# Second attention of a two-block kernel: forget decays as row products of running sums instead of masked decay matrices

## What is computed

```python
qh = rms_norm(heads(q), q_gain); kh = rms_norm(heads(k), k_gain)
logf = jax.nn.log_sigmoid(f_logit + f_bias)          # (B, S, 8)
c = jnp.cumsum(logf, axis=1).transpose(0, 2, 1)      # running sum over tokens
s = einsum('bhtd,bhsd->bhts', qh, kh) * scale
s = s + c[:, :, t, None] - c[:, :, None, s]          # decay between key s and query t
s = where(t >= s, s, -inf); pr = softmax(s); o = pr @ v
```

## Time and profile before

| what | value |
|---|---|
| median of 3 runs | 912.39 us (912.27 to 912.58) |
| the profiled execution's own time | 910.87 us |
| its span in the profile | 909.2 us |
| mean granted clock of TensorE | 0.994 of full speed |
| the stretch of this change in the profile | about 564 to 633 us |

### The profile page before, as it was taken

One profiled execution on the slowest core, in us unless ns is written; L12 is line 12 of the kernel. 1 busy time (PEld: TensorE's weight loads), 2 busy tenths in 40 slices (PEclk: granted clock), 3 DMA queues, 4 the chain that ended last, 5 costly groups with the idle time before them and its releaser, 6 DMA issues.

```text
span 909.2 us, 16558 instructions
## 1 busy us (share of the span) xinstructions
PE 879.7 (97%) x7228; PEld 816.3 (90%) x7228; DVE 626.8 (69%) x758; ACT 482.7 (53%) x578; POOL 43.9 (5%) x66
## 2 busy tenths in 40 slices
PE   8999899998988999999999999989999999999997
PEld 8988899998878999999979888989989999999986
DVE  6879477697938855478887886985466555555564
ACT  5657723647426744367776454565545443443463
POOL 5000150000000000000000000131000000000000
PEclk9999999999988999999999999999999999999999
DMA  9846210324108974579965443351454655555521
GB/s 256 278 167 205 79 50 3 140 94 139 47 1 297 388 270 164 186 271 368 351 207 186 144 161 112 126 195 50 142 185 152 228 188 188 183 185 190 181 93 47
DMA packets 88905, 156.75 MB, mean 172 GB/s; under 512 B 7432, under 2 KB 61184, under 8 KB 84864
## 3 DMA queue, kind: packets, MB, share of 16 engines
q1 hardware_dynamic: 88144, 154.90, 49.4%
q10 hardware_dynamic: 688, 0.79, 0.3%
HBM read 154.62 MB, written 1.05 MB: 171 GB/s over the span
## 4 chain that ended last, share of the span: by engine, by line
PE 76%; DVE 15%; ACT 4%; SPq 2%; issue 2%; DMA 1%; POOL 0%; DVEq 0%; POOLq 0%; ACTq 0%
PE ps L1053 8%; PE ps L1056 8%; PE ps L1055 8%; PE ps L1108 7%; PE ps L1109 7%; PE ps L1110 7%; DVE w_lo L1833 5%; PE ps L1541 4%; PE ps L1539 4%; PE ps L1540 4%; PE ps L1307 3%; PE ps L1611 2%; PE ps L1612 2%; PE ps L1613 2%; ACT w_hi L564 2%
## 5 line engine op out<-in xcount | busy, mean ns | idle before, releaser
L1833 DVE TENSOR_TENSOR w_lo<-raw,w_hi 128x2048 fp32r<-128x2048 f32 (+2 forms) x148 | 334.6, 2266 | 136.5 <-ACT w_hi L564 135.2
L564 ACT ACTIVATE w_hi<-raw 128x2048 fp32r<-128x2048 f32 (+2 forms) x148 | 277.8, 1881 | 81.1 <-PE ps L1110 27.5
L1053 PE MATMUL ps<-h_hi,w_hi 128*128 128x256 f32 x736 | 210.5, 286 | 4.2 <-ACT arena L672 1.6
L1055 PE MATMUL ps<-h_lo,w_hi 128*128 128x256 f32 x736 | 208.2, 283 | 0.0
L1056 PE MATMUL ps<-h_hi,w_lo 128*128 128x256 f32 x736 | 208.2, 283 | 0.0
L1053 PEld LDWEIGHTS ps<-h_hi,w_hi 128*128 128x128 f32 x736 | 141.0, 192 | 6.9 <-issue 3.9
L1055 PEld LDWEIGHTS ps<-h_lo,w_hi 128*128 128x128 f32 x736 | 141.1, 192 | 0.4
L1056 PEld LDWEIGHTS ps<-h_hi,w_lo 128*128 128x128 f32 x736 | 141.0, 192 | 0.0
L1108 PE MATMUL ps<-w_hi,h_hi 128*128 128x512 f32 (+1 forms) x240 | 93.9, 391 | 0.5 <-DVE h_lo L2242 0.5
L1539 PE MATMUL ps<-w_hi,arena_rounded 128*128 128x256 f32 x320 | 92.1, 288 | 0.7 <-DVE w_lo L1833 0.6
L1109 PE MATMUL ps<-w_lo,h_hi 128*128 128x512 f32 (+1 forms) x240 | 92.6, 386 | 0.0
(11 more groups left out here) (449 smaller groups left out, 1391.4 us busy)
## 6 DMA issues: line engine op xcount, KB each, us to landing
raw<-in_w_in SPq DMA_DIRECT2D x35, 1024.0 KB, 5.1
raw<-in_w_exp_up SPq DMA_DIRECT2D x16, 1024.0 KB, 4.9
raw<-in_w_exp_down SPq DMA_DIRECT2D x16, 1024.0 KB, 4.9
raw<-in_w_exp_gate SPq DMA_DIRECT2D x15, 1024.0 KB, 5.0
raw<-in_w_ffn_gate SPq DMA_DIRECT2D x11, 1024.0 KB, 5.2
raw<-in_w_ffn_up SPq DMA_DIRECT2D x11, 1024.0 KB, 5.1
raw<-in_w_ffn_down SPq DMA_DIRECT2D x11, 1024.0 KB, 4.9
raw<-in_w_out SPq DMA_DIRECT2D x8, 1024.0 KB, 5.0
```

The source lines that it names most:

```text
L564: act.activation(w_hi[:, j % SPL, 0:kt * n], raw[:, j % RAW, 0:kt * n], ACT.Copy).then_inc(w_high, 1)
L1053: pe.matmul(o, hi[:, k, cols], a_hi[:, k, :], start=(k == 0 and (whole or c == 0)), stop=False)
L1055: pe.matmul(o, hi[:, k, cols], a_lo[:, k, :], start=False, stop=False)
L1833: dve.tensor_tensor(w_lo[:, j % SPL, 0:kt * n], raw[:, j % RAW, 0:kt * n], w_hi[:, j % SPL, 0:kt * n].bitcast(F32), sub).then_inc(w_ready, 1)
```

## The change

The running sums over the tokens are computed once, as rows (one row per head, 256 tokens), by three fp32 matmuls, and a copy of them goes into rows 0 to 7 and 32 to 39 of a tile `decay_rows`. The copy by ACT rounds them to fp32r; DVE then replaces rows 32 to 39 by what the rounding lost. `pick[:, h]` is a column that is -1 at rows h and 32+h, so that one fp32r product per head and query tile adds minus the running sum of the keys to the logits. The part that belongs to the query is left out, since the softmax cancels it. `f_mask` and its products go. PE computes the sums behind gate chunk 3 (into bank 2). ACT's root for `o_norm` moves behind the Silu, the four head copies and `gate_out(2)`, and the copy of the sums stands behind the root. DVE gets three small instructions ahead of the softplus and one more behind it.

```diff
@@ ScalarE
             gate_out(GATE2, 1, gate2, s_gate_ev2)
-            act.wait_ge(s_ors, 2)
-            act.activation(nrm[:, :, 0:4], nrm[:, :, 0:4], ACT.Sqrt).then_inc(s_orr, 1)
             act.activation(z2[:, :, Z2_G:Z2_G + 512], z2[:, :, Z2_G:Z2_G + 512],
                            ACT.Silu).then_inc(s_zs, 1)
             for j in range(4):
                 act.wait_ge(s_fq_ps, j + 1)
                 act.activation(qk2_t[:, 2 * j:2 * j + 2, :], split3(bank((4, 5, 0, 1)[j]), 2),
                                ACT.Copy).then_inc(s_fq, 1)
             gate_out(GATE2, 2, gate2, s_gate_ev2)
+            act.wait_ge(s_ors, 2)
+            act.activation(nrm[:, :, 0:4], nrm[:, :, 0:4], ACT.Sqrt).then_inc(s_orr, 1)
+            act.wait_ge(s_cols_ps, 2)
+            act.activation(decay_rows[0:40], bank(2)[0:40, 0:S], ACT.Copy).then_inc(s_cols, 1)
             gate_out(GATE2, 3, gate2, s_gate_ev2)
@@ TensorE
             gate_chunk(GATE2, 3, s_gate_ev2)
+            pe.wait_ge(s_frows, 1)
+            pe.wait_ge(s_hg_ev, 3)
+            pe.matmul(bank(2)[0:40, 0:P], glog_twice[:, 0, :], upto[:, :], start=True, stop=True)
+            pe.matmul(bank(2)[0:40, P:S], glog_twice[:, 0, :], ones[:, :], start=True, stop=False)
+            pe.matmul(bank(2)[0:40, P:S], glog_twice[:, 1, :], upto[:, :], start=False, stop=True).then_inc(s_cols_ps, 1)
             gate_chunk(GATE2, 4, s_gate_ev2)
             pe.wait_ge(s_on, 2)
+            pe.wait_ge(s_frows, 2)
             turn_out(ho, 2)
             gate_chunk(GATE2, 5, s_gate_ev2)
             pe.wait_ge(s_fq, 4)
-            pe.wait_ge(s_fmask, 1)
+            pe.wait_ge(s_frows, 2)
...
                         o = split3(bank(j), len(hs))[:, n, :]
-                        if t == 1:
-                            pe.matmul(o[:, 0:P], ones[:, :], f_mask[:, 0, h, :], start=False, stop=False)
-                            pe.matmul(o[:, 0:P], upto[:, :], last(glog[:, 1, h], P),
-                                      start=False, stop=False)
                         own = o[:, P * t:P * t + P]
-                        pe.matmul(own, upto[:, :], f_mask[:, t, h, :], start=False, stop=False)
+                        pe.matmul(o, last(pick[:, h], P), decay_rows[:, 0:P * (t + 1)], start=False, stop=False)
                         m = pe.matmul(own, ident_bf[:, :], future_bf[:, :], start=False, stop=(n == len(hs) - 1))
@@ VectorE
             step(dve.tensor_scalar(sp1, sp1, -1.0, None, mult))
+            dve.scalar_tensor_tensor(pick[:, :], ident[:, 0:8], -1.0, ident[:, 32:40], mult, sub)
+            dve.memset(decay_rows.bitcast(F32), 0.0)
+            step(dve.memset(glog_twice, 0.0))
             softplus(1, 3)
             ahead(LVL2[7])
-            step(dve.tensor_scalar(glog, sp1, -1.0, None, mult))
+            for first in (0, 32):
+                m = dve.tensor_scalar(glog_twice[:, :, first:first + 8], sp1, -1.0, None, mult)
+            m.then_inc(s_frows, 1)
...
             o_norm(ho, hsq, 1, HG_HEADS, HG_D, rep[:, C_ONORM:C_ONORM + HG_D], z2[:, :, Z2_G:Z2_G + 512],
                    lambda: ahead(GATE2[2]))
-            for t in range(NT):
-                m = dve.tensor_tensor(f_mask[:, t], mid(after[:, :], 8), last(glog[:, t], P), mult)
-            m.then_inc(s_fmask, 1)
+            dve.wait_ge(s_cols, 2)
+            dve.tensor_tensor(decay_rows[32:40], bank(2)[32:40, 0:S], decay_rows[32:40].bitcast(F32),
+                              sub).then_inc(s_frows, 1)
             ahead(GATE2[3])
             ahead(GATE2[4])
```

More of the change, by code:

```diff
@@ L189, in two_block_program @@
         order_i = sb("order_i", [P, N_GROUPS], I32)
+        pick = sb("pick", [P, 8], F32R)
         with nc.sbuf_tensor("arena_rounded", [P, 21460], F32R) as arena_rounded:
@@ L282, in two_block_program @@
         qk2_t = view(5136, 8, S)
-        f_mask = view(7184, NT, HEADS, P)
+        decay_rows = view(7184, S, of=arena_rounded)
         prob2 = view(9232, NT, HEADS, S)
@@ L321, in two_block_program @@
         top8b = small[:, 464:472]
+        glog_twice = split3(small[:, 536:616], 2)
         gain_mix = small[:, 456:464]
@@ L392, in two_block_program @@
             "forget_logits_in_sbuf", "gate_logits_in_sbuf", "gate_logits_in_sbuf_2"))
-        (s_fq_ps, s_fq, s_fmask, s_fl_ps, s_p_ps, s_p_hi, s_p_ready, s_plg,          s_result, s_out) = (sem(n) for n in (
-            "fox_heads_in_psum", "fox_heads_ready", "forget_operand", "fox_logits_in_psum",
+        (s_fq_ps, s_fq, s_frows, s_fl_ps, s_p_ps, s_p_hi, s_p_ready, s_plg,          s_result, s_out) = (sem(n) for n in (
+            "fox_heads_in_psum", "fox_heads_ready", "forget_rows", "fox_logits_in_psum",
             "p_turned", "p_high", "p_ready", "ple_gate_ready",
```

## The result

The changed kernel takes 903.18 us (median of 4 runs, 902.36 to 903.72) against 912.34 us for the kernel before beside it (4 runs, 912.27 to 912.58): a ratio of 0.9899, with an interval of 0.9886 to 0.9912. The profiled execution took 902.36 us with a span of 900.6, where before it was 910.87 and 909.2.

The account below looks back on a forecast made before the run. PE, busy 97% of the span, was taken as the bound: 4.8 us won in the logits plus 1.65 us ahead of them made 6.4 us, taking the median from 912.39 to 906.0 us, range 904.9 to 908.9.

Parts of the forecast that it names:

- these two waits: PE ahead of the logits: 1.6 us waiting for `gate_out(2)` on ACT and 1.0 us for a `w_lo` split.
- What bounds the kernel: Whole kernel: PE is busy 97% of the span, so work taken from it pays nearly in full.
- The new sums on PE: Behind gate chunk 3: three fp32 products, six instructions, cost PE 0.77 us; lower bound 0.4.
- DVE ahead of the softplus: Small new DVE instructions take 0.5 us, up to 0.7; PE starts chunk 3 0.45 us late.
- ACT's new order: ACT ahead of chunk 4: PE's 1.6 us wait goes; the root's extra 1.28 us table load is hidden by 0.4.
- The chain of the new rows: From PE's sums through ACT and DVE to chunk 5: `w_lo` of `GATE2[5]` ends at 600.5 instead of 602.9.
- The GpSimd hit that I gave `o_norm`: DVE's `o_norm` product: GpSimd's gate product would slow it by 1.1 us, so it ends at 597.8.
- The logits: PE's logits: one fp32r product per head and tile wins 4.8 us, bounds 4.2 and 5.3.
- the 256-column price: Logits, query tile 0: the 128-column fp32r product priced at 0.255 us a head, winning 0.6 us.
- B: Ahead of the logits: DVE stays the bound, chunk 5 gains 0 to 1 us; about -4.5, 907.9 us; chance 0.21.
- C: Behind the logits: softmax or branch merging comes last, PE keeps about 2 us, giving 910.4; chance 0.08.
- D: In the logits: the one-column-broadcast fp32r product is slow; 0.5 us more each gives 914; chance 0.05.

Follow-up runs that it names:

- e5: The changed kernel with DVE's three set-up instructions moved ahead of its wait for ACT's last level decay; 904.0 us.
- e4: The kernel before with ACT's new order alone (root behind the Silu, head copies and `gate_out(2)`); 912.15 us, ratio 1.0001.
- e3: The changed kernel with ACT's old order, the root first; 904.71 us, ratio 0.9918.
- e0: The kernel before, unchanged, profiled and timed once more; 911.34 us, ratio 0.9993.
- e1: The kernel before plus only the unused 32-byte tile `pick` ahead of the arena; 910.61 us, ratio 0.9984.
- e2: The changed kernel with `pick` inside the arena, so that the arena lies where it lay before; 905.19 us, ratio 0.9927.
- e12: The changed kernel, unchanged, measured once more beside the kernel before; 903.03 us, ratio 0.9896.
- e7: The kernel before with a 64-byte pad ahead of the arena, so it again starts 32 past a multiple of 64; 909.7 us.
- e8: The changed kernel with `pick` inside the arena and a 64-byte pad ahead of the token tiles; 904.26 us.
- e6: The changed kernel with `pick` ahead of the token tiles instead of the arena, moving them by 32 bytes; 903.68 us.

## Why the prediction was wrong

Its mechanism held step by step, in the stretch that it looked at. The step that failed is "So three things can be won: PE time in the logits, and at most these two waits ahead of them": a fourth lay outside the stretch, the pitch of the experts' matmuls. Beside it one term of the sum, the fp32r product of 128 columns, was priced too high. What came out wrong is the size: 8.5 us in the profiled execution (910.87 to 902.36) where it said 6.4, and 9.2 in the medians.

- **What bounds the kernel, the waits.** Right. PE paid in full, and both waits ahead of the logits went. Chunk 3, chunk 4, `turn_out` and chunk 5 started within 0.1 us of the forecast, counted from the common start.
- **The new sums on PE, DVE ahead of the softplus.** Right: 0.78 for 0.77 and 0.56 for 0.5. e5 gives the second its price in time, 0.4 for 0.45.
- **ACT's new order.** Right in what it does, too high in what it is worth by itself. The table load ahead of the root is hidden, by 0.2 us rather than 0.4 (591.06 against 591.26; the reciprocal also has a `w_lo` split ahead of it that ends then). But the order was worth 0.8 us (e4, e3), not the 1.6 that the wait lasted: without it the new sums run inside the wait. The sum of the forecast holds, since it counts the wait as won and the sums as paid. The Trainium skill ("ScalarE: Activation LUTs", What ACT_TABLE_LOAD costs) adds a drain of some 1.38 us to a switch of tables; the rows show ACT's split copy until 589.54, the load from 589.55 for 1.28 us and the root from 590.85, directly behind it. The trace agrees with the load and not with the drain.
- **The chain of the new rows.** The GpSimd hit that I gave `o_norm` did not come: its last product took 1.23 us, although GpSimd's gate product began at 594.34. GpSimd itself took 2.12 us for it instead of 1.30, and the two `w_lo` splits behind took 5.03 where two alone take 2 x 2.29 = 4.6. So the subtraction was done at 595.75 and not, with the lead taken off, at 596.8. It had cover in either case, and the time does not depend on it.
- **The logits: the step that failed inside the stretch.** "I take the 256-column price" for the fp32r product of 128 columns, 0.255 a head. It measured 0.19, which is the lower bound that the prediction had worked out. Over four heads it is (607.91 - 607.16) / 4 = 0.1875, which makes 8 x (0.255 - 0.1875) = 0.54 us; tile 1, at (612.84 - 611.85) / 4 = 0.248, gives 0.06 more. The argument that weight loads of this width follow each other no faster was taken from fp32 rows, and it does not hold for fp32r behind bf16. With this term at 5.45 and the 1.70 ahead of it the tail is -7.15; the trace has -7.19. The prediction's own range for this mechanism was added up 0.2 us short: 6.4 + 0.5 + 0.45 + 0.37 is 7.7 and not 7.5, and its other end is -5.55 and not -5.2. The tail lies inside either.
- **The step that was missing, and that put the time outside the range.** The change was taken to touch only the stretch from 564 to 633, and everything ahead of it was put at nothing. It also declares a tile, and the tile lies ahead of the arena that the experts' matmuls read. That was worth 1.6 us in the experts (1.3 between e0 and e1, 1.4 between e2 and e12), less 0.24 us by which the start of the kernel was later. e2, the same change with the arena in its old place, measured 905.19 us, inside the range. The forecast's rows hold nothing on what the place of a tile does; that the change declares a tile ahead of the arena can be read in its code.
- **The rest.** The forecast median took the distance of the profiled execution from the median of before, 1.5 us, along; after it was 0.8. So 2.8 = 0.8 (tail) + 1.4 (experts less start, and 0.06 of the scan's stretch) + 0.7 (this distance), with 0.1 lost between span and time. The last is spread: the same kernel's profiled spans were 900.6 and 902.1 in the first measurement and in e12, and 1.35 of these 1.5 us lie ahead of the placement copy (289.07 and 290.42), where the mean granted clock from 265 to 285 was 0.74 and 0.66.
- **The rivals.** B did not come: no wait for a `w_lo` at chunk 5. C is refuted by the 287.8 us from chunk 6 to the end in both kernels. D had it the wrong way round: the row product with the broadcast weight is at the lowest price that was thought possible.

Still open is why a shift of 32 or 64 bytes changes the pitch of a matmul. The boundary of 64 bytes (e7) and the distances within 128 (e8) are refuted as the rule, and no other was tried.

GpSimd's products of the changed kernel, in its timeline:

```profile
587.82 1.30 POOL L546 TENSOR_TENSOR arena<-arena 128x512 f32<-128x512 f32 x1 [5.92 <-ACT arena L674]
594.34 2.12 POOL L546 TENSOR_TENSOR arena<-arena 128x512 f32<-128x512 f32 x1 [5.22 <-ACT arena L674]
```

The second is the one that met DVE's product and splits.

## What to carry to other kernels

A new tile is part of a change: see which tiles lie behind it and which matmuls read them, and when comparing two kernels, first subtract what they differ by ahead of the changed code. Price a short matmul of a faster type from its own bounds and not from the rows of a slower type. A wait that is removed by order alone comes back in part at the next engine that was nearly late (e4: 1.6 us gone, 1.0 us back), so don't count it at its full length. And when two profiles of one kernel differ, compare the granted clock by stage before looking for a cause in the code.

## What was not expected of the hardware

- The place of a tile in SBUF changes the pitch of the matmuls that read it, by one to three per cent: 121.2 ns between starts against 119.2 for the experts' products when the arena moves by 32 bytes (e0, e1; the durations go from 286, 283 and 281 ns to 283, 280 and 280), and 120.2 to 117.0 for 256 columns but 229.5 to 234.6 for 512 when the token tiles move (changed kernel, e6).
- An fp32r product of 128 columns between bf16 products costs 0.15 us with what the two changes of type cost (607.16 to 607.31) where the fp32 one costs 0.28 (608.96 to 609.24); at 256 columns 0.21 against 0.48.
- A table load on ACT begins 0.01 us behind the instruction ahead of it and is followed by its activation within 0.02 us (587.59 + 1.95, 589.55 + 1.28, 590.85).
- The same code was 1.35 us slower ahead of the placement copy where the granted clock was lower for longer: 0.66 on average from 265 to 285 us (e12) against 0.74 (the first profile of the changed kernel).
